# Output projection's first tile pulled forward between attention heads, and the work around it re-ordered

## The chip, the cores and the metric

The kernel runs on one core of one Trainium2 chip. The metric is the device time of the whole program in microseconds. Four compute engines work side by side, each through its own instructions in program order: TensorE (PE, with its weight loads PEld), VectorE (DVE), ScalarE (ACT) and GpSimd (POOL). SyncE (SP) only issues weight transfers. They wait for one another by counting semaphores.

## The reference, cut to what matters

Two blocks of two layers each are computed for 256 tokens of width 1024 in float32. The change lies in the first block's first layer, the attention mixer, and in the output projection behind it (shortened, with the normalisations left out):

```
z = h @ w_in
...
o_mla = blocked_causal_attention(q, k, v_mla, MLA_QK ** -0.5)         # 8 heads, rms-normed q and k, rope
o_fox = blocked_causal_attention(qf, kf, vf, FOX_DIM ** -0.5, cum_log_f)  # 8 heads, forget gates
h = h + concatenate([o_mla, o_fox]) @ w_out
h = h + sq_relu_mlp(rms_norm(h, g_mlp), w_mlp_up, w_mlp_down)
```

Each MLA query row carries a normalising factor, (mean of squares) ** -0.5, for each head. The log_sigmoid of a vector `lam` belongs to the second block, much later.

## The kernel before

Every matrix product is done in float32 by three passes: the weights are split into a high part `whi` (ACT, a copy of `raw` in a rounded format) and a low part `wlo` (DVE, `raw` minus `whi`), the activations likewise (`xhi` and `xlo`, or `chi` and `clo` for the attention's output), and TensorE adds hi·hi, hi·lo and lo·hi in one bank of `ps`. A **unit** is 8 blocks of 128x128 weights, which is one output tile of 128 features: 24 matmuls of 258 columns here. `whi` and `wlo` have 4 slots; ACT and DVE split a unit three units ahead of its use (LA = 3): the helper `ahead`, called at unit j, splits unit j + 3, and DVE's split waits for ACT's.

**The head steps.** 18 items (`items`) go through a software pipeline: 16 heads ("h", 0 to 7 fox, 8 to 15 MLA) and two small items ("d") for the first queries. In step `st` TensorE computes the scores of item st, transposes the probabilities of item st-2 (`turn`) and multiplies item st-3 by the values (`values`). DVE takes the row maximum (`peak`, L1468) and divides by the sum (`normal`, L1491), ACT takes the exponential (`exps`, L1883) and copies the transposes back (`turned`, L1913). Items use two banks of scores in turn, so scores(j) wait for the exponential of j-2. The results of a pair of heads become one block of `chi` (`high`) and `clo` (`low`, L1497).

In the same steps the MLA keys and queries are finished. `key_spread(i)` (L963) is one matmul into bank 7, which waits for DVE's `k_normed` of pair i-1 (L1454, L1458), since that still reads the bank. `q_stats` are small matmuls for the queries' sums of squares, one part each in `turn(1)` to `turn(5)`. ACT copies them out, POOL forms the mean, ACT's `query_power` raises it to -0.5 by a Ln and an Exp, and POOL refines it (`q_scale`); the first MLA item cannot be scaled before.

**The output projection** (`attn_out`, units 24 to 31). After the last scores `out_blocks` computes blocks 0 to 5 of tiles 0, 1 and 2 between the last steps, then block 6 and block 7 of the three, as these become available, then tiles 3 to 7 whole. DVE adds each tile to `h` (`dve_residual`, L552), ACT makes `xhi` and the squares from it (`act_residual`), DVE makes `xlo` (L508). The next phase, `mlp0_up`, takes block b of its first tile when `xlo` of tile b is there.

Of the kernel before, what the change touches and what calls it, by code (L numbers as in the profile page):

```python
# [19 lines left out]
F32R = mybir.dt.float32r  # L20
ACT = mybir.ActivationFunctionType
# [127 lines left out]
def program(nc, x_in, w8, w6, params_in, consts_in, rows_in, pad_in, ws_in, bs_in, out):  # L149
# [3 lines left out]
    with ctx:  # L153
# [384 lines left out]

        def dve_residual(dve, p, segs, n, c0, t):
# [255 lines left out]
        def tile_bank(t):  # L795
# [112 lines left out]
        def _(pe):  # L908
# [236 lines left out]
            def turn(j):  # L1145
# [73 lines left out]
            def out_blocks(j, kts):  # L1219

                u = p_out.unit0 + j
                o = ps[:, j % 4, 0:T1]
# [11 lines left out]
            for st in range(4, NIT + 3):  # L1234
                if st < NIT:
                    scores(st)
                if st in KEY_SPREAD:
                    key_spread(KEY_SPREAD[st])
                if st < NIT + 2:
                    turn(st - 2)  # L1240
                if items[st - 3][0] == "h":
                    values(items[st - 3][1])
                if st >= NIT:
                    j = st - NIT
                    if j < 2:
                        pe.wait_ge(ex_done, parts_done(NIT - 1 + j))
                    else:
                        pe.wait_ge(pt_done, NHD - 1)
                    out_blocks(j, range(KT - 2))
# [138 lines left out]
        def _(dve):  # L1388
# [71 lines left out]

            def peak(j):
# [8 lines left out]
                if j == 1 + HEADS:  # L1470
                    dve.wait_ge(q_scale, 6)
                    nc.vector.tensor_reduce(q_d[0:META, 0:1], q_diag[0:META, :], AX.X, ALU.add).then_inc(q_scale, 1)
# [33 lines left out]
            def step(st):  # L1506
                if st < NIT:
                    peak(st)
                if 1 <= st <= NIT:
                    normal(st - 1)  # L1510
                if st in KEY_FINAL:
# [96 lines left out]
            for _ in dve_log_sigmoid(dve, par("lam", 0, NB), half_lam[:, :], tmp[:, 0, 0:NB], tmp[:, 1, 0:NB],  # L1608
                            tmp[:, 0, NB:2 * NB], s("lam_step"), s("lam_exp_asked"), s("lam_exp")):
# [4 lines left out]

# [897 lines left out]
```

## Time and profile before

| | us |
|---|---|
| median of 3 runs | 1332.41 (1332.26 to 1333.31) |
| the profiled execution | 1332.28, span 1330.5 |
| TensorE busy | 1302.3, 98% of the span |
| head steps 4 to 17 on TensorE | 101.4 to 147.1 |
| output projection until the next phase's first tile is done | 147.1 to 177.8 |

Times within the span are counted from its first instruction. In the timeline rows the second number is how long an instruction, or a merged run of them, took; the number in brackets is the engine's idle time just before it, with the instruction that released it. Matmuls are pipelined: the next one starts before the former is finished, so their pace is read from starts.

### The profile page before, as it was taken

Reading aid. Unit: us, or ns where it says so; the run is one execution under the profiler, and the core shown is the slowest. Engines: PE = TensorE matmul, PEld = TensorE weight load, DVE = VectorE, ACT = ScalarE, POOL = GpSimd, SP = SyncE. Lnnn points to the kernel's source line nnn. Section 1 sums busy time; section 2 is a strip of 40 time slices with the busy share of each in tenths; the row PEclk is TensorE's granted clock in tenths of the full one; section 3 lists DMA queues with packets and bytes.
Section 4 is the critical chain, followed back from the end, with each engine's and each line's share of the span. In section 5 each row is a group of like instructions: output and inputs, shape, how many; then the busy total and the mean of one; then the engine's idle time right before and its main releaser. Section 6 shows DMA issues by size and latency. Waiting matters only on the chain. (4 is left out here: it accounts for less than half of the span.)

```text
span 1330.5 us, 28216 instructions
## 1 busy us (share of the span) xinstructions
PE 1302.3 (98%) x10550; PEld 1274.0 (96%) x10550; DVE 953.9 (72%) x1426; ACT 743.5 (56%) x1192; POOL 342.7 (26%) x374
## 2 busy tenths in 40 slices
PE   9998999999999999999999999999999989999997
PEld 8987899999999999999899999999999989999996
DVE  6867787655487776655455669998559898999844
ACT  5555554444343554444556556666457886666542
POOL 4632133310011233200006214343103022434311
PEclk9999999999999999999999999999999999999998
DMA  9520155555555455555545545554564445555451
GB/s 307 187 100 1 67 188 190 189 191 180 174 185 188 159 190 189 190 187 177 205 158 186 190 155 199 188 182 147 186 214 173 169 167 198 205 183 180 158 191 55
DMA packets 35370, 230.50 MB, mean 173 GB/s; under 512 B 4062, under 2 KB 5214, under 8 KB 11910
## 3 DMA queue, kind: packets, MB, share of 16 engines
q1 hardware_dynamic: 34228, 226.99, 48.6%
q10 hardware_dynamic: 1058, 2.38, 0.5%
q8 instruction: 54, 0.88, 0.3%
q14 instruction: 30, 0.25, 0.1%
HBM read 228.17 MB, written 1.05 MB: 172 GB/s over the span
## 5 line engine op out<-in xcount | busy, mean ns | idle before, releaser
L392 DVE TENSOR_TENSOR wlo<-raw,whi 128x1024 fp32r<-128x1024 f32 (+1 forms) x446 | 525.5, 1182 | 104.7 <-ACT whi L386 102.2
L427 PE MATMUL ps<-xhi,whi 128*128 128x256 f32 (+2 forms) x1920 | 542.9, 283 | 4.9 <-DVE wlo L392 3.9
L428 PE MATMUL ps<-xlo,whi 128*128 128x256 f32 (+2 forms) x1920 | 542.0, 282 | 0.0
L429 PE MATMUL ps<-xhi,wlo 128*128 128x256 f32 (+2 forms) x1920 | 540.8, 282 | 0.0
L386 ACT ACTIVATE whi<-raw 128x1024 fp32r<-128x1024 f32 (+2 forms) x444 | 446.8, 1011 | 153.3 <-PE ps L429 135.7
L427 PEld LDWEIGHTS ps<-xhi,whi 128*128 128x128 f32 x1920 | 362.4, 189 | 8.6 <-issue 5.6
L429 PEld LDWEIGHTS ps<-xhi,wlo 128*128 128x128 f32 x1920 | 362.9, 189 | 0.0
L428 PEld LDWEIGHTS ps<-xlo,whi 128*128 128x128 f32 x1920 | 360.7, 188 | 0.3
L427 PE MATMUL ps<-hhi,whi 128*128 128x256 f32 (+1 forms) x1184 | 334.3, 282 | 2.0 <-issue 0.8
L429 PE MATMUL ps<-hhi,wlo 128*128 128x256 f32 (+1 forms) x1184 | 333.2, 281 | 0.0
L428 PE MATMUL ps<-hlo,whi 128*128 128x256 f32 (+1 forms) x1184 | 333.0, 281 | 0.0
L427 PEld LDWEIGHTS ps<-hhi,whi 128*128 128x128 f32 x1184 | 223.6, 189 | 3.6 <-issue 1.9
L428 PEld LDWEIGHTS ps<-hlo,whi 128*128 128x128 f32 x1184 | 223.5, 189 | 0.0
L429 PEld LDWEIGHTS ps<-hhi,wlo 128*128 128x128 f32 x1184 | 223.4, 189 | 0.0
L534 POOL TENSOR_TENSOR ssum<-ssum,sq 128x256 f32<-128x256 f32 (+1 forms) x63 | 48.8, 774 | 393.4 <-ACT sq L515 393.4
L714 POOL TENSOR_TENSOR work<-work 128x256 f32<-128x256 f32 x48 | 66.2, 1378 | 176.5 <-ACT work L670 171.0
L552 DVE TENSOR_TENSOR h<-ps,h 128x256 f32<-128x256 f32 (+3 forms) x56 | 23.7, 424 | 115.6 <-PE ps L429 115.2
L685 ACT ACTIVATE work<-tmp,params 128x256 f32<-128x256 f32 x96 | 57.7, 601 | 87.0 <-DVE tmp L655 87.0
L628 POOL TENSOR_TENSOR hlo<-act,hhi 128x258 f32 (+1 forms) x64 | 66.7, 1042 | 119.4 <-ACT hhi L620 119.4
L503 ACT ACTIVATE xhi<-h,params 128x256 fp32r<-128x256 f32 (+1 forms) x56 | 28.6, 511 | 88.8 <-DVE h L552 83.3
L620 ACT ACTIVATE hhi<-act 128x258 fp32r<-128x258 f32 (+3 forms) x64 | 26.9, 420 | 88.1 <-DVE act L607 88.1
L646 DVE SCALAR_TENSOR_TENSOR work<-tmp,params,work 128x254 f32<-128x254 f32 x96 | 53.6, 558 | 10.4 <-DVE work L643 0.3
(339 smaller groups left out, 1338.1 us busy)
## 6 DMA issues: line engine op xcount, KB each, us to landing
raw<-w SPq DMA_DIRECT2D x182, 1024.0 KB, 4.9
raw<-w SPq DMA_DIRECT2D x40, 768.0 KB, 4.2
raw<-w SPq DMA_DIRECT2D x4, 512.0 KB, 5.4
h<-x_fm ACTq DMA_DIRECT2D x4, 272.0 KB, 5.6
out_fm<-h SPq DMA_DIRECT2D x6, 128.0 KB, 1.9
ws<-ws_src ACTq DMA_DIRECT2D x1, 512.0 KB, 3.5
bs<-bs_rows ACTq DMA_DIRECT2D x1, 512.0 KB, 5.0
consts<-constants SPq DMA_DIRECT2D x1, 508.0 KB, 10.4
```

The costliest lines, as they stand in the source:

```text
L386: nc.scalar.activation(whi[:, w, 0:n], raw[:, slot, col:col + n], ACT.Copy).then_inc(whi_done, 3 if lead else 1)
L392: nc.vector.tensor_tensor(wlo[:, w, 0:n], raw[:, slot, col:col + n], whi[:, w, 0:n].bitcast(F32), ALU.subtract).then_inc(wlo_done, 3 if fr ...
L427: nc.tensor.matmul(o, hi, xh, start=start, stop=False)
L428: nc.tensor.matmul(o, hi, xl, start=False, stop=False)
L429: mm = nc.tensor.matmul(o, lo, xh, start=False, stop=stop)
L503: nc.scalar.activation(xhi[:, kt, c0:c0 + t], h[:, kt, c0:c0 + t], ACT.Identity, scale=par(NORM_GAIN[n], kt)).then_inc(xhi_done, 1)
L534: nc.gpsimd.tensor_tensor(ssum[:, c0:c0 + t], ssum[:, c0:c0 + t], sq[:, slot, 0:t], ALU.add).then_inc(ssum_done, 1)
L620: nc.scalar.activation(hi[:, k, 0:t], src[:, j % 2, 0:t], ACT.Copy).then_inc(uhi_done, 1)
L628: nc.gpsimd.tensor_tensor(lo[:, k, 0:t], src[:, j % 2, 0:t], hi[:, k, 0:t].bitcast(F32), ALU.subtract).then_inc(ulo_done, 1)
L646: nc.vector.scalar_tensor_tensor(out=c[:, 2:SEQ], in0=x[:, 0:SEQ - 2], scalar=w0, in1=c[:, 2:SEQ], op0=ALU.mult, op1=ALU.add).then_inc(who ...
L685: nc.scalar.activation(cb[:, j % 4, :], tmp[:, j % 2, 0:SEQ], ACT.Identity, scale=par(f"f_conv_w{layer}", it * (3 * UB) + 3 * j + 2), bias ...
L714: nc.gpsimd.tensor_tensor(half[:, i % 2, :], gg[:, i % 2, :], cb[:, (2 * i + 1) % 4, :], ALU.mult).then_inc(u_done, 1)
```

## The change

1. The item list takes the first MLA head ("h", 8) before the second small item ("d", 1); the other MLA heads follow behind it.
2. `query_power` moves from ACT (Ln, Exp) to DVE (an integer first guess and two Newton steps, 8 instructions of 24 columns), in step 7. The parts of `q_stats` are done in four turns in place of five, and POOL waits for DVE's eighth instruction.
3. `key_spread` comes behind `turn` and `values` in its step, and the last one, with its `k_normed`, moves from step 7 to step 8.
4. Blocks 0 to 3 of output tile 0 run in steps 15, 16 and 17 (one, two, one), in bank 7, which the key spreads have left. Only blocks 4 and 5 stay where all six were.
5. In `dve_residual` of `attn_out` the split of the unit three ahead comes before the addition of the tile, not between the addition and `xlo`.
6. All of the `lam` log_sigmoid but its first two instructions moves behind `mlp0_up`.

```diff
+            return 7 if j == 0 else j % 4
...
                 for j in range(UB):
                     if j % segs != segs - 1:
+                        ahead(dve, split_lo, p, it, j, last)
+                    if p.name == "attn_out":
                         ahead(dve, split_lo, p, it, j, last)
                     if j % segs == segs - 1:
...
-                        nc.vector.tensor_tensor(hh, ps[:, jt % ring + (4 - ring), 0:t], hh,
+                        bank = out_bank(jt) if p.name == "attn_out" else jt % ring + (4 - ring)
+                        nc.vector.tensor_tensor(hh, ps[:, bank, 0:t], hh,
                                                 ALU.add).then_inc(tile_free, 1)
-                        ahead(dve, split_lo, p, it, j, last)
+                        if p.name != "attn_out":
+                            ahead(dve, split_lo, p, it, j, last)
                         if n != 8:
                             dve_xlo(dve, n, kt, c0, t)
...
-        items = ([("d", 0)] + [("h", i) for i in range(HEADS)] + [("d", 1)]
-                 + [("h", HEADS + i) for i in range(HEADS)])
+        items = ([("d", 0)] + [("h", i) for i in range(HEADS + 1)] + [("d", 1)]
+                 + [("h", HEADS + i) for i in range(1, HEADS)])
...
+        OUT_EARLY = {15: (0,), 16: (1, 2), 17: (3,)}
-        KEY_SPREAD = {5: 1, 6: 2, 7: 3}
-        KEY_FINAL = {4: 0, 5: 1, 6: 2, 7: 3}
+        KEY_SPREAD = {5: 1, 6: 2, 8: 3}
+        KEY_FINAL = {4: 0, 5: 1, 6: 2, 8: 3}
...
-                if 1 <= j < 6:
-                    q_stats(j - 1)
-                if j == 6:
+                for part in {1: (0,), 2: (1,), 3: (2, 3), 4: (4,)}.get(j, ()):
+                    q_stats(part)
+                if j == 5:
                     pe.wait_ge(s("q_stats_out"), 2)
...
-                if st in KEY_SPREAD:
-                    key_spread(KEY_SPREAD[st])
                 if st < NIT + 2:
                     turn(st - 2)
                 if items[st - 3][0] == "h":
                     values(items[st - 3][1])
+                if st in KEY_SPREAD:
+                    key_spread(KEY_SPREAD[st])
+                if st in OUT_EARLY:
+                    if 0 in OUT_EARLY[st]:
+                        pe.wait_ge(k_out, 4 * HEADS // 2)
+                    out_blocks(0, OUT_EARLY[st])
...
-                    out_blocks(j, range(KT - 2))
+                    out_blocks(j, range(4 if j == 0 else 0, KT - 2))
...
+            def query_power():
+
+                c, y, z, mean = s("q_power"), q_inv[:, :, :], q_neg[:, :, :], q_part[:, 0:3, :]
+                yi = y.bitcast(I32)
+                dve.wait_ge(s("q_mean"), 1)
+                nc.vector.tensor_scalar(yi, mean.bitcast(I32), 1, None, ALU.logical_shift_right).then_inc(c, 1)
+                dve.wait_ge(c, 1)
+                nc.vector.tensor_scalar(yi, yi, -1, 0x5F3759DF, ALU.mult, ALU.add).then_inc(c, 1)
+                for k in range(2):
+                    dve.wait_ge(c, 3 * k + 2)
+                    nc.vector.tensor_tensor(z, y, y, ALU.mult).then_inc(c, 1)
...
-                nc.scalar.activation(q_neg[:, :, :], q_part[:, 0:3, :], ACT.Ln).then_inc(s("q_log"), 1)
-                act.wait_ge(s("q_log"), 1)
-                nc.scalar.activation(q_inv[:, :, :], q_neg[:, :, :], ACT.Exp, scale=-0.5).then_inc(s("q_power"), 1)
...
-            pool.wait_ge(s("q_power"), 1)
+            pool.wait_ge(s("q_power"), 8)
```

How the order of instructions moves on DVE at the output projection, in the kernel before: `wlo` is the low part of a weight unit, `h` the residual sum of a tile, `xlo` the low part of that tile's activations, and `half_lam` and `params` end the log_sigmoid.

```order
L1611 TENSOR_SCALAR half_lam<-tmp 128x12 [waits lam_step]
L1612 TENSOR_SCALAR params<-params 128x24
L552 TENSOR_TENSOR h<-ps,h 128x258 [waits unit_done]
L392 TENSOR_TENSOR wlo<-raw,whi 128x1024 [waits whi_done]
L508 SCALAR_TENSOR_TENSOR xlo<-h,params,xhi 128x258 [waits xhi_done]
L552 TENSOR_TENSOR h<-ps,h 128x258 [waits unit_done]
L392 TENSOR_TENSOR wlo<-raw,whi 128x1024 [waits whi_done]
L508 SCALAR_TENSOR_TENSOR xlo<-h,params,xhi 128x258 [waits xhi_done]
```

The same place on DVE in the changed kernel:

```order
L748 SCALAR_TENSOR_TENSOR tmp<-params 128x12 [waits params_loaded]
L751 COPY half_lam<-tmp 128x12 [waits lam_step]
L393 TENSOR_TENSOR wlo<-raw,whi 128x1024 [waits whi_done]
L560 TENSOR_TENSOR h<-ps,h 128x258 [waits unit_done]
L509 SCALAR_TENSOR_TENSOR xlo<-h,params,xhi 128x258 [waits xhi_done]
L393 TENSOR_TENSOR wlo<-raw,whi 128x1024 [waits whi_done]
L560 TENSOR_TENSOR h<-ps,h 128x258 [waits unit_done]
L509 SCALAR_TENSOR_TENSOR xlo<-h,params,xhi 128x258 [waits xhi_done]
```

The sum of a tile now stands behind a split, where it stood ahead of it, and the log_sigmoid is gone from in front of the first sum. ACT's own order there is the same in both kernels, here as the changed one has it:

```order
L387 ACTIVATE whi<-raw 128x1024 [waits unit_done,raw_full1]
L504 ACTIVATE xhi<-h,params 128x258 [waits tile_free]
L516 ACTIVATE sq<-h 128x258 [waits ssum_done]
L387 ACTIVATE whi<-raw 128x1024 [waits unit_done,raw_full2]
L504 ACTIVATE xhi<-h,params 128x258 [waits tile_free]
L516 ACTIVATE sq<-h 128x258 [waits ssum_done]
```

Nothing moved here: the high part of the next unit still stands behind `xhi` and `sq` of the tile, and `xhi` waits for `tile_free`, which the sum `h` counts up.

On TensorE, steps 15 and 16 of the changed kernel (L1238 to L1240 are `out_blocks`, L1150 and L1152 scores, L1186 transposes, L1201 to L1205 values):

```order
L1238 MATMUL ps<-chi,whi 128x258 [waits olo_done,wlo_done,k_normed]
L1239 MATMUL ps<-clo,whi 128x258
L1240 MATMUL ps<-chi,wlo 128x258
L1150 MATMUL ps<-k_mla,q_mla 128x144 [waits k_normed,q_normed,exp_done]
...
L1205 MATMUL ps<-extra,v_early 128x258 [waits d_turned]
L1238 MATMUL ps<-chi,whi 128x258 [waits olo_done,wlo_done]
L1239 MATMUL ps<-clo,whi 128x258
L1240 MATMUL ps<-chi,wlo 128x258
L1238 MATMUL ps<-chi,whi 128x258 [waits olo_done]
```

In the kernel before, the scores follow the values there at once:

```order
L1191 MATMUL ps<-extra,v_main 128x258 [waits prob_t_done]
L1192 MATMUL ps<-extra,v_main 128x128
L1195 MATMUL ps<-extra,v_early 128x258 [waits d_turned]
L1140 MATMUL ps<-k_mla,q_mla 128x144 [waits k_normed,q_normed,exp_done]
L1142 MATMUL ps<-mask_r 128x128
```

So three or six matmuls of the output projection now stand ahead of the scores of items 16 and 17, and three ahead of the transposes of item 16.

## Rows read from the trace of the kernel before

**Rows 1.** Page, busy time, share of the span and instructions of each engine

```profile
PE 1302.3 (98%) x10550; PEld 1274.0 (96%) x10550; DVE 953.9 (72%) x1426; ACT 743.5 (56%) x1192; POOL 342.7 (26%) x374
```

**Rows 2.** Timeline of TensorE, head steps (start us, us, what, idle before)

```profile
106.75 0.39 PE L963 MATMUL ps<-inv,sel 128*128 128x272 f32 x1 [1.40 <-DVE k_mla L1458]
...
123.39 0.70 PE L1191 MATMUL ps<-extra,v_main 128*128 128x258 f32 x2 [2.09 <-ACT extra L1913]
...
126.89 0.41 PE L1140 MATMUL ps<-k_mla,q_mla 96*128 96x144 f32 x2
...
153.03 0.60 PE L1191 MATMUL ps<-extra,v_main 128*128 128x258 f32 x2
```

**Rows 3.** Timeline of VectorE, its waits in the head steps

```profile
112.00 0.66 DVE L1468 TENSOR_REDUCE soft<-ps 128x1 f32<-128x144 f32 x2 [1.88 <-PE ps L1142]
...
121.46 0.43 DVE L1497 TENSOR_TENSOR clo<-ps,chi 128x258 fp32r<-128x258 f32 x1 [0.76 <-ACT chi L1919]
...
123.13 0.15 DVE L1472 TENSOR_REDUCE q_d<-q_diag 16x1 f32<-16x8 f32 x1 [1.07 <-POOL q_neg L2284]
...
125.67 0.65 DVE L1468 TENSOR_REDUCE soft<-ps 128x1 f32<-128x144 f32 x2 [1.36 <-PE ps L1142]
...
127.97 0.66 DVE L1468 TENSOR_REDUCE soft<-ps 128x1 f32<-128x144 f32 x2 [0.79 <-PE ps L1142]
```

**Rows 4.** Timeline of ScalarE, its query_power

```profile
118.10 1.28 ACT L1834 ACT_TABLE_LOAD   x1
...
120.93 0.22 ACT L1836 ACTIVATE q_inv<-q_neg 128x24 f32<-128x24 f32 x1
```

**Rows 5.** Timeline of TensorE, output projection and next phase's first tile

```profile
157.63 0.28 PE L1230 MATMUL ps<-chi,wlo 128*128 128x258 f32 x1
...
160.49 0.39 PE L1228 MATMUL ps<-chi,whi 128*128 128x258 f32 x1 [1.86 <-DVE wlo L392]
...
177.53 0.39 PE L427 MATMUL ps<-xhi,whi 128*128 128x258 f32 x1
```

**Rows 6.** Timeline of VectorE, log_sigmoid, output projection, next phase

```profile
155.78 0.17 DVE L726 TENSOR_SCALAR tmp<-half_lam 128x12 f32<-128x12 f32 x1 [0.28 <-ACT half_lam L2007]
...
156.87 1.19 DVE L732 SCALAR_TENSOR_TENSOR tmp<-tmp 128x12 f32<-128x12 f32 x6
...
158.88 0.42 DVE L552 TENSOR_TENSOR h<-ps,h 128x258 f32<-128x258 f32 x1
159.22 1.22 DVE L392 TENSOR_TENSOR wlo<-raw,whi 128x1024 fp32r<-128x1024 f32 x1
160.35 0.87 DVE L508 SCALAR_TENSOR_TENSOR xlo<-h,params,xhi 128x258 fp32r<-128x258 f32 x1
161.14 0.41 DVE L552 TENSOR_TENSOR h<-ps,h 128x258 f32<-128x258 f32 x1
...
175.13 0.43 DVE L552 TENSOR_TENSOR h<-ps,h 128x258 f32<-128x258 f32 x1 [0.38 <-PE ps L1230]
...
186.15 1.23 DVE L392 TENSOR_TENSOR wlo<-raw,whi 128x1024 fp32r<-128x1024 f32 x1 [0.64 <-ACT whi L386]
```

**Rows 7.** Timeline of ScalarE, output projection and next phase

```profile
159.33 0.51 ACT L503 ACTIVATE xhi<-h,params 128x258 fp32r<-128x258 f32 x1 [2.64 <-DVE h L552]
...
160.06 1.04 ACT L386 ACTIVATE whi<-raw 128x1024 fp32r<-128x1024 f32 x1
...
185.07 1.05 ACT L386 ACTIVATE whi<-raw 128x1024 fp32r<-128x1024 f32 x1
```

**Rows 8.** Windows A:B: length, busy (x) of PE PEld DVE ACT POOL, clock, DMA

```profile
108.00:111.00 3.00, 3.00 (x12) 2.62 (x11) 2.03 (x5) 1.33 (x6) 0.00 (x0) 0.50 0.00 0
...
126.89:147.10 20.21, 17.76 (x114) 14.91 (x113) 15.86 (x54) 16.28 (x51) 2.81 (x9) 1.00 0.13 44
...
1323.00:1324.00 1.00, 0.00 (x0) 0.00 (x0) 1.00 (x2) 0.00 (x0) 0.61 (x2) 0.55 0.00 0
```

**Rows 9.** Timeline of TensorE, its last matmuls

```profile
1321.05 0.70 PE L1384 MATMUL ps<-sq,consts 128*128 128x256 f32 x2 [0.54 <-ACT sq L515]
```

More of the change, by code:

```diff
@@ L20 @@
 F32R = mybir.dt.float32r
+I32 = mybir.dt.int32
 ACT = mybir.ActivationFunctionType
@@ L535, in pool_ssum, with out_bank @@
                                     ALU.add).then_inc(ssum_done, 1)
+        def out_bank(j):
+            return 7 if j == 0 else j % 4
         def dve_residual(dve, p, segs, n, c0, t):
@@ L1221, in out_blocks @@
                 u = p_out.unit0 + j
-                o = ps[:, j % 4, 0:T1]
+                o = ps[:, out_bank(j), 0:T1]
                 pe.wait_ge(wlo_done, u + 1)
@@ L1242, in _ @@
                     values(items[st - 3][1])
+                if st in KEY_SPREAD:
[4 more added lines that the diff above has]
+                    out_blocks(0, OUT_EARLY[st])
                 if st >= NIT:
                     j = st - NIT
-                    if j < 2:
-                        pe.wait_ge(ex_done, parts_done(NIT - 1 + j))
-                    else:
+                    if j == 1:
+                        pe.wait_ge(ex_done, parts_done(NIT))
+                    if j == 2:
                         pe.wait_ge(pt_done, NHD - 1)
-                    out_blocks(j, range(KT - 2))
+                    out_blocks(j, range(4 if j == 0 else 0, KT - 2))
             for j in range(3):
@@ L1459, in k_normed @@
                                         ALU.mult).then_inc(k_out, 1)
+            def query_power():
[8 more added lines that the diff above has]
+                    nc.vector.tensor_tensor(z, y, y, ALU.mult).then_inc(c, 1)
+                    dve.wait_ge(c, 3 * k + 3)
+                    nc.vector.scalar_tensor_tensor(out=z, in0=z, scalar=-0.5, in1=mean, op0=ALU.mult,
+                                                   op1=ALU.mult).then_inc(c, 1)
+                    dve.wait_ge(c, 3 * k + 4)
+                    nc.vector.scalar_tensor_tensor(out=y, in0=z, scalar=1.5, in1=y, op0=ALU.add,
+                                                   op1=ALU.mult).then_inc(c, 1)
             def peak(j):
@@ L1471, in peak @@
                     dve.wait_ge(q_scale, 6)
+                if j == D1:
                     nc.vector.tensor_reduce(q_d[0:META, 0:1], q_diag[0:META, :], AX.X, ALU.add).then_inc(q_scale, 1)
@@ L1510, in step @@
                     normal(st - 1)
+                if st == 7:
+                    query_power()
                 if st in KEY_FINAL:
@@ L1607, in _ @@
             dve.wait_ge(s("params_loaded"), 16)
-            for _ in dve_log_sigmoid(dve, par("lam", 0, NB), half_lam[:, :], tmp[:, 0, 0:NB], tmp[:, 1, 0:NB],
-                            tmp[:, 0, NB:2 * NB], s("lam_step"), s("lam_exp_asked"), s("lam_exp")):
+            lam = dve_log_sigmoid(dve, par("lam", 0, NB), half_lam[:, :], tmp[:, 0, 0:NB], tmp[:, 1, 0:NB],
+                            tmp[:, 0, NB:2 * NB], s("lam_step"), s("lam_exp_asked"), s("lam_exp"))
+            next(lam)
+            dve_residual(dve, ph["attn_out"], 1, 1, C1, T1)
+            dve_rstd(dve, 1, C1, T1, ph["mlp0_up"])
+            dve_mlp_up(dve, ph["mlp0_up"], C1, T1)
+            for _ in lam:
                 pass
@@ L1613, in _ @@
                                     ALU.mult).then_inc(s("gate_bias_done"), 1)
-            dve_residual(dve, ph["attn_out"], 1, 1, C1, T1)
-            dve_rstd(dve, 1, C1, T1, ph["mlp0_up"])
-            dve_mlp_up(dve, ph["mlp0_up"], C1, T1)
             dve_residual(dve, ph["mlp0_down"], 4, 2, C1, T1)
@@ L1829, in to @@
                     done[0] += 1
-            def query_power():
-                act.wait_ge(s("q_mean"), 1)
-                nc.scalar.activation(q_neg[:, :, :], q_part[:, 0:3, :], ACT.Ln).then_inc(s("q_log"), 1)
-                act.wait_ge(s("q_log"), 1)
-                nc.scalar.activation(q_inv[:, :, :], q_neg[:, :, :], ACT.Exp, scale=-0.5).then_inc(s("q_power"), 1)
             def roots(n):
@@ L1904, in turned @@
                                          ACT.Copy).then_inc(pt0_done, 1)
-                if j == 5:
+                if j == 4:
                     nc.scalar.activation(q_part[:, :, :], ps[:, 6, 2 * P:2 * P + 4 * HEADS].rearrange(
@@ L1926, in step @@
                     turned(st - 2)
-                if st == 7:
-                    query_power()
                 if st >= 3 and second(st - 3) and items[st - 3][1] < HEADS:
```

## The prediction

> **What bounds the kernel now.** I read the page's busy times first: TensorE is busy 1302.3 of 1330.5 us [rows 1]. A change of order can only win what TensorE stands idle or runs slowly, and it loses as soon as it makes new idle time. So I went to the timeline of TensorE over the edited stretch and looked for its waits. In the head steps there are several: 1.40 us for the key norms at 106.75 and 2.09 us for ACT's copy at 123.39 [rows 2]. Then I looked at what DVE waits for in the same steps [rows 3], since it does more small work there than the others, and at what holds ACT: two table loads, from 118.10 to 121.15 [rows 4]. From 147.1 on TensorE runs without a gap until 158.6, waits 1.86 us for the low weight part of the fourth tile, and has no gap again until the next phase's first tile is done [rows 5]. The reader should keep the last view in mind: between 160.49 and 177.53 TensorE issues 5 tiles of 24 matmuls and 7 blocks of 3, 141 in 17.04 us, which is 0.121 us each and **2.9 us for a tile**. Whatever feeds it there must be faster than that.
>
> **The change, part by part.**
>
> *Split before the sum in the output projection (part 5).* Before, DVE adds tile j, splits unit j+3 while ACT makes xhi and the squares of tile j and the high part of unit j+4, and then makes xlo. Its pace was 161.14 - 158.88 = 2.26 us a tile [rows 6], less than TensorE's 2.9. The rows of order show that ACT's order is untouched: the high part of unit j+4 stands behind xhi of tile j, which waits for the sum of tile j. With the split of unit j+4 now ahead of the sum of tile j+1, everything stands in one chain: sum(j), xhi(j), squares(j), high(j+4), low(j+4), sum(j+1). From starts in the rows: sum to xhi 159.33 - 158.88 = 0.45; xhi to high part 160.06 - 159.33 = 0.73 [rows 6, 7]; high part to the low part that waits for it 186.15 - 185.07 = 1.08 [rows 6, 7]; low part to DVE's next instruction 160.35 - 159.22 = 1.13 [rows 6]. The sum is **3.39 us a tile, slower than TensorE's 2.9**. No row of before shows the chain closed like this, but each link of it stands in one, and nothing in it is optional.
>
> What it costs is read at the last block of the next phase's first tile, which needs xlo of tile 7. Before: tile 0 is finished at 157.63 + 0.28 = 157.91 and that block starts at 177.53 [rows 5], 19.6 us later, the stall of 1.86 us included. After: the first sum follows tile 0 at once (0.05), seven periods are 23.7, then sum to xhi 0.45, xhi 0.51, xlo 0.87, and 0.07 for two hand-overs: 25.7 us. **Loss 6.1 us.** Most of it is no stall between tiles: TensorE itself would be through tile 7 about 17 us after tile 0, and then waits for xlo of tiles 5, 6 and 7, each a period behind the other. For tiles 4 to 7 the low weight parts come 0.5 us late each, and the rest, twice about 3 us, is waited ahead of the last two blocks.
>
> *The log_sigmoid moved (part 6).* Its 3.1 us from 155.78 to 158.88 stood in front of the first sum and of the split that TensorE waits 1.86 us for [rows 5, 6]. Gone from there, the split of the fourth tile is done before tile 0 is. That win of 1.86 is already inside the 6.1, since I counted from one end to the other. Behind mlp0_up the same 3 us are hidden by splits three units ahead, 8.7 us of TensorE; without that cover they would cost 3.1.
>
> *Head steps up to the second MLA head (parts 1 to 3).* I count in DVE's idle time, because its work there is fixed and nearly without a gap. Before, from 106.7 to the peak of head 9 at 127.97, it waits 1.88 + 0.76 + 1.07 + 1.36 + 0.79 = 5.86 us [rows 3]: for scores behind the late key spread, for ACT behind its table loads, for POOL's scale behind the same, and for two scores that follow from it. The table loads go entirely, 3.0 us of ACT. Into DVE's line come the 8 new instructions. Nothing in the trace is a shift or an integer product, but the chain of small dependent ones nearest to it takes 1.19 / 6 = 0.2 us each [rows 6], so 1.6; the bounds are nothing more than 1.0 and 2.4 us. New waits: the key spread of pair 1 now stands behind a transpose and a values product, which puts it about 0.65 us behind the point where DVE wants it, and I leave 1.1 us of the waits for scores, because scores follow exponentials and those are not faster. 5.86 - 1.6 - 0.65 - 1.1 = **2.5 us won**, bounds 1.0 and 4.2 (none of the new waits). In this the clock counts too: after the wait of 1.40 us TensorE ran at half clock from 108 to 111 [rows 8]. With the spread at the end of the step that wait is gone, and I take it that the fall is gone with it.
>
> *Heads 9 to 15 and the early blocks (part 4).* From 126.89 to 147.10 TensorE is idle 20.21 - 17.76 = 2.45 us [rows 8]. Four blocks of 0.36 us, 1.44 us in all, are put there, and go from behind 147.1. They do not simply fill gaps: the scores of items 16 and 17 stand behind them and DVE's peak waits for scores, so part of the 1.44 pushes the chain. Step by step, the first block is taken up by the gap before the next values, the next two push by 0.7 to 0.8, the last falls into a gap: about 0.6 won. The short item now between heads 8 and 9 lets ACT catch up, where it ran two full exponentials ahead of a copy, for another 0.8. **1.4 us won**, bounds 0 and 2.45.
>
> Both together bring the last values product, 153.03 before [rows 2], forward by **3.9 us**, and behind it the order is fixed up to tile 0's end.
>
> *The clock.* In the stretch of loss TensorE would be idle for 3 us, do 0.36 us, be idle for 3 us again. At the end of the program the granted clock had fallen from 2.4 to 1.2 GHz by 1323 to 1324, 2 us after the last matmuls [rows 8, 9], and in the head steps it fell behind an idle stretch of 1.40. The row at half clock covers 3.00 us of a busy TensorE, so it gave up 1.5 us, and with its edges somewhat more. I add **1.8 us** for one such fall; bounds 0 and 3.
>
> Sum, against the profiled execution's own 1332.28, which is 0.13 below the median: 1332.3 + 6.1 - 3.9 + 1.8 = 1336.3; I say 1336.2.
>
> Two rules of the skill bear on this. The Trainium skill, "ScalarE: Activation LUTs", section "What ACT_TABLE_LOAD costs", gives 1283 ns for a load and about as much again for a drain, 2.66 us for a switch. The load agrees with 1.28 here, but the next instruction starts at once, so no row here shows the drain; by the page's figure the two loads would be worth 5.3 us of ACT and not 2.6, and the head steps could win up to 2.7 us more. The Trainium skill, "TensorE: Matmul & The Clock Gate", section "Architectural detail", says that ScalarE and VectorE are strict first in, first out, which speaks against this change: ACT cannot start the next high part ahead of a waiting xhi. The trace agrees, ACT idles 2.64 us ahead of xhi with the next high part behind it.
>
> **The rivals.**
>
> *The chain does not bind; the change is faster.* If ACT had the next high part ready, the period would stay under 2.9, and only the wins would be left: 1332.3 - 3.9 - 1.86 = 1326.5. The deciding point is a period of 2.9 us: three links of 0.45, 1.08 and 1.13 are hand-overs that can't shrink by 0.5 together, so I give it 1 in 20. The same side is reached if the head steps win more than 6.1 us; their upper bounds are 4.2 + 2.45 = 6.65. 1 in 20.
>
> *The clock does not fall.* The wait of 2.09 us that ended at 123.39 was not followed by half-rate matmuls [rows 2], so an idle stretch alone does not bring the fall each time. Then 1334.4, within 0.2%. 1 in 4.
>
> *The head steps win less.* If the clock still falls among them (1.5), or DVE's integer instructions cost 2.4, or the early blocks only push, 3.9 becomes about 2: 1338.2. 3 in 20.
>
> *The forecast* itself has 1 in 2.
>
> **How the numbers follow.** What a measurement of this kernel can tell from no change is about 0.2%, 2.7 us. Slower than 1335.1: forecast and the last rival, 0.65. Within: the rival without a fall, 0.25. Faster than 1329.7: 0.10. The range leaves out the two cases on the fast side and the far end of the last rival: low 6.1 - 5.2 + 0 = 0.9, high 6.1 - 2.2 + 1.8 = 5.7, so 1333.2 to 1338.0.
>
> **What would show it.** In the trace after: sums of the output projection 3.4 us apart, not 2.26; TensorE waits of about 0.5 us for the low weight part ahead of tiles 5, 6 and 7, and two of about 3 us for xlo in the next phase's first tile; half clock right behind. No Ln and no table load in the head steps; eight small DVE instructions of 0.2 us; the last values product near 149.1. The prediction is wrong if the sums come 2.9 us apart or less, or if the last values product stands earlier than 147 or later than 151.

## The result, and the profile after

| | us |
|---|---|
| before, median of 7 runs | 1332.41 (1330.17 to 1333.31) |
| after, median of 7 runs | 1337.43 (1336.28 to 1338.86) |
| ratio after / before | 1.0042, 95% interval 1.003 to 1.0053 |
| the profiled execution of after | 1338.36, span 1336.6 |

The change makes the kernel 5.0 us slower. The forecast was 1336.2, with a range of 1333.2 to 1338.0: the sign is right and the time lies in the range, but the step from before was put at 3.8 us, which is less than the interval of the ratio allows (4.0 to 7.1).

VectorE in the timeline of the changed kernel, from the first split to the third tile (start, duration, what, idle before). It answers to [rows 6]:

```profile
155.54 1.23 DVE L393 TENSOR_TENSOR wlo<-raw,whi 128x1024 fp32r<-128x1024 f32 x1 [1.23 <-ACT whi L387]
156.76 0.43 DVE L560 TENSOR_TENSOR h<-ps,h 128x258 f32<-128x258 f32 x1
157.76 0.49 DVE L509 SCALAR_TENSOR_TENSOR xlo<-h,params,xhi 128x258 fp32r<-128x258 f32 x1 [0.58 <-ACT xhi L504]
159.02 1.23 DVE L393 TENSOR_TENSOR wlo<-raw,whi 128x1024 fp32r<-128x1024 f32 x1 [0.77 <-ACT whi L387]
160.16 0.42 DVE L560 TENSOR_TENSOR h<-ps,h 128x258 f32<-128x258 f32 x1
161.16 0.49 DVE L509 SCALAR_TENSOR_TENSOR xlo<-h,params,xhi 128x258 fp32r<-128x258 f32 x1 [0.58 <-ACT xhi L504]
162.42 1.23 DVE L393 TENSOR_TENSOR wlo<-raw,whi 128x1024 fp32r<-128x1024 f32 x1 [0.77 <-ACT whi L387]
163.56 0.42 DVE L560 TENSOR_TENSOR h<-ps,h 128x258 f32<-128x258 f32 x1
...
180.56 0.42 DVE L560 TENSOR_TENSOR h<-ps,h 128x258 f32<-128x258 f32 x1
```

The sums are 3.40 us apart, to the last one at 180.56. DVE now waits twice in each tile, 0.58 us for `xhi` and 0.77 us for `whi`, where it had hardly a gap before: it isn't the engine that sets the pace. ScalarE in the same place, which answers to [rows 7], closes the circle:

```profile
160.62 0.51 ACT L504 ACTIVATE xhi<-h,params 128x258 fp32r<-128x258 f32 x1 [1.63 <-DVE h L560]
161.04 0.40 ACT L516 ACTIVATE sq<-h 128x258 f32<-128x258 f32 x1
161.35 1.04 ACT L387 ACTIVATE whi<-raw 128x1024 fp32r<-128x1024 f32 x1
```

ScalarE waits 1.63 us for `h`, DVE's split waits for `whi`, and `h` stands behind the split. The links, by starts: 160.16 to 160.62, to 161.35, to 162.42, to 163.56, which is 0.46 + 0.73 + 1.07 + 1.14 = 3.40.

TensorE from the last values product to the statistics of the next phase (L472), which answers to [rows 5] and to the last row of [rows 2]:

```profile
151.84 0.60 PE L1201 MATMUL ps<-extra,v_main 128*128 128x258 f32 x2
...
163.75 0.36 PE L1238 MATMUL ps<-chi,whi 128*128 128x258 f32 x1 [0.27 <-issue]
167.15 0.36 PE L1238 MATMUL ps<-chi,whi 128*128 128x258 f32 x1 [0.27 <-issue]
...
178.70 0.39 PE L428 MATMUL ps<-xhi,whi 128*128 128x258 f32 x1 [2.37 <-DVE xlo L509]
182.10 0.58 PE L428 MATMUL ps<-xhi,whi 128*128 128x258 f32 x1 [2.77 <-DVE xlo L509]
182.91 0.42 PE L428 MATMUL ps<-xhi,whi 128*128 128x258 f32 x1
...
187.34 0.60 PE L472 MATMUL ps<-ssum,consts 128*128 128x258 f32 x2
```

The big waits are not where the tiles are computed but ahead of the last two blocks of the next phase's first tile, 2.37 and 2.77 us. The matmul behind 182.91 takes 0.42 us and not 0.28: the clock is down. Windows of the same profile (length, busy of PE, PEld, DVE, ACT, POOL, then the granted clock, DMA share, GB/s) show it twice, in the head steps and behind the loss; they answer to [rows 8]:

```profile
104.00:105.00 1.00, 1.00 (x9) 0.82 (x10) 0.96 (x3) 0.00 (x0) 0.86 (x2) 0.74 0.00 0
...
106.00:107.00 1.00, 1.00 (x5) 0.81 (x4) 0.97 (x4) 0.95 (x5) 0.84 (x1) 0.50 0.00 0
...
180.00:186.00 6.00, 3.90 (x18) 3.91 (x19) 2.69 (x4) 3.05 (x4) 0.64 (x1) 0.50 0.41 137
```

And VectorE in the head steps: the key norms' wait for the spread, and the first two of the eight instructions that replace Ln and Exp.

```profile
111.68 0.49 DVE L1468 SCALAR_TENSOR_TENSOR k_mla<-early,params,ps 64x272 f32<-64x272 f32 x1 [1.59 <-PE ps L973]
...
118.85 0.17 DVE L1480 TENSOR_SCALAR q_inv<-q_part 128x24 int32<-128x24 int32 x1
119.06 0.18 DVE L1482 TENSOR_SCALAR q_inv<-q_inv 128x24 int32<-128x24 int32 x1
```

Five marks let every profile be split into stretches: the first `q_stats` matmul, the last values product, the first sum, the last block of the next phase's first tile, and the statistics matmul behind it. Start times in us, of all profiled executions (the labels are those of the experiments below). The last column has the microseconds in which the granted clock was at or near half:

| profile | q_stats | last values | first sum | last block | statistics | clock fell to half |
|---|---|---|---|---|---|---|
| before | 100.00 | 153.03 | 158.88 | 177.53 | 180.88 | 108 to 111 |
| e5 (before) | 102.22 | 154.40 | 160.25 | 180.45 | 183.78 | 125 to 129, 163 to 167 |
| e10 (before) | 101.75 | 157.40 | 163.26 | 181.92 | 185.26 | 109 to 119 |
| after | 101.50 | 151.84 | 156.76 | 182.10 | 187.34 | 105 to 108, 180 to 186 |
| e9 (after) | 101.32 | 149.99 | 154.90 | 180.24 | 185.85 | 179 to 185 |
| e1 | 101.96 | 150.64 | 155.55 | 174.21 | 177.55 | none |
| e2 | 101.34 | 154.39 | 161.38 | 186.72 | 192.10 | 110 to 112, 185 to 191 |
| e3 | 100.84 | 150.26 | 155.18 | 180.53 | 186.40 | 180 to 186 |
| e4 | 102.56 | 151.22 | 156.13 | 173.99 | 177.32 | none |
| e6 | 100.93 | 150.33 | 155.24 | 173.12 | 176.44 | none |
| e7 | 100.63 | 151.61 | 156.52 | 174.38 | 177.70 | 124 to 127 |
| e8 | 100.56 | 152.90 | 157.81 | 175.68 | 179.01 | 108 to 114 |
| e11 | 101.10 | 153.31 | 158.23 | 176.89 | 180.23 | 124 to 128 |
| e12 | 102.49 | 151.15 | 156.06 | 179.25 | 184.10 | 180 to 182 |

The last column tells of 101 to 192 us alone. What lies behind the statistics is 1149.1 to 1149.8 us in every one of them, so nothing of the change acts there; the log_sigmoid in its new place costs nothing that can be seen.

### The profile page after: what moved, and what is told of

Read it like the earlier page. It is cut to its first block and busy times, and to the rows that moved or that the text cites. A ratio compares the mean times of both kernels' runs of the same rounds, so it can differ in the third digit from the quotient of the medians.

```text
span 1336.6 us, 28222 instructions
## 1 busy us (share of the span) xinstructions
PE 1305.1 (98%) x10550; PEld 1275.7 (95%) x10550; DVE 952.5 (71%) x1434; ACT 740.0 (55%) x1188; POOL 344.3 (26%) x374
## 5 line engine op out<-in xcount | busy, mean ns | idle before, releaser
(340 smaller groups left out, 1334.2 us busy)
```

## The experiments

They were run in three groups, each beside its own runs of the kernel before: e1 to e4 (before 1332.13, 13 runs), e5 to e8 (1333.31, 19 runs), e9 to e12 (1333.15, 23 runs).

**e1, the sum first again.** The changed kernel without its part 5.

```diff
-                    if p.name == "attn_out":
-                        ahead(dve, split_lo, p, it, j, last)
...
-                        if p.name != "attn_out":
-                            ahead(dve, split_lo, p, it, j, last)
+                        ahead(dve, split_lo, p, it, j, last)
```

> The changed kernel with one part undone: in the output projection DVE again adds the tile before it splits the unit three ahead. All else is as changed. If the closed chain of 3.4 us a tile is the loss (my theory), the sums come 2.3 us apart until they meet TensorE's pace, the two waits of about 3 us for xlo in the next phase's first tile go, the half clock behind them goes too, and one wait of about 1.1 us for the low part of the fourth tile comes back: about 8 us faster than the changed kernel, 1329 to 1330 us, ratio to before 0.997 to 0.998. If the loss came from the moved log_sigmoid or from the early blocks, this would stay near 1337.

Measured: 1328.16 (1326.39 to 1328.91), ratio 0.996, interval 0.9946 to 0.9974. The sums are 2.26 us apart again:

```profile
155.55 0.43 DVE L558 TENSOR_TENSOR h<-ps,h 128x258 f32<-128x258 f32 x1 [2.45 <-PE ps L1237]
155.90 1.22 DVE L393 TENSOR_TENSOR wlo<-raw,whi 128x1024 fp32r<-128x1024 f32 x1
157.03 0.87 DVE L509 SCALAR_TENSOR_TENSOR xlo<-h,params,xhi 128x258 fp32r<-128x258 f32 x1
157.82 0.41 DVE L558 TENSOR_TENSOR h<-ps,h 128x258 f32<-128x258 f32 x1
```

First sum to last block takes 18.66 us instead of 25.34, and the clock stays up behind it. One place in DVE's order is worth 9.3 us, and all the rest of the change together is a win of 4.0 us.

**e2, the split first alone.** The kernel before with part 5 and nothing else.

```diff
+                    if p.name == "attn_out":
+                        ahead(dve, split_lo, p, it, j, last)
...
-                        ahead(dve, split_lo, p, it, j, last)
+                        if p.name != "attn_out":
+                            ahead(dve, split_lo, p, it, j, last)
```

> The kernel before with this one part done: the split three ahead stands before the sum of the tile in the output projection. The log_sigmoid is still in front of the first sum. Theory: the chain runs from the end of that first split, about 160.0, seven periods of 3.4 and 1.9 more: the next phase's first tile ends near 185.7 and not 177.5, 8 us later, and the clock falls behind it for another 1.5: 1341 to 1342 us. Rival, that the order of DVE costs nothing by itself: 1332.

Measured: 1341.55 (1339.91 to 1343.0), ratio 1.0062, interval 1.0047 to 1.0076; that is 9.4 us more than before. First sum to last block is 25.34 us, to a hundredth what the whole change has, and the clock falls behind it too. The loss belongs to part 5 alone.

**e3, no early blocks.** The changed kernel with all six blocks of tile 0 where they were.

```diff
-        OUT_EARLY = {15: (0,), 16: (1, 2), 17: (3,)}
+        OUT_EARLY = {}
...
-                    out_blocks(j, range(4 if j == 0 else 0, KT - 2))
+                    if j == 0:
+                        pe.wait_ge(k_out, 4 * HEADS // 2)
+                    out_blocks(j, range(KT - 2))
```

> The changed kernel with blocks 0 to 3 of output tile 0 back behind the last scores, still in bank 7. Theory: the four blocks were worth 0.6 us in the head steps, so this is 0.6 slower than the changed kernel, about 1338.0. Rival A, they fill gaps entirely: 1.4 slower. Rival B, they only push the scores: no difference, or faster. The last values product tells it in the trace more closely than the time does.

Measured: 1337.23 (1336.19 to 1338.6), ratio 1.0032, interval 1.0021 to 1.0043. By the time alone the kernel without the early blocks is 0.2 us faster and not 0.6 slower, which is below what the time can tell. By the stretches, `q_stats` to last values product is 49.42 us. In the first profile of after it is 50.34, but with the clock down for a while; so e6 and e9 were made for this.

**e4, the split first for one tile.** Part 5 kept for tile 0, where DVE waits for it anyway, and the old order for the other seven.

```diff
-                    if p.name == "attn_out":
+                    if p.name == "attn_out" and j == 0:
...
-                        if p.name != "attn_out":
+                        if p.name != "attn_out" or j > 0:
```

> The changed kernel with the split ahead of the sum for the first tile alone; from the second tile on DVE adds first and splits then. Theory: the wait of 1.1 us for the fourth tile's low part that the plain order has goes as well, and nothing else changes against it: 1328 to 1329 us, 9 us faster than the changed kernel and about 1 us faster than with the plain order. Rival, the first closed link delays the second tile's split as well: equal to the plain order.

Measured: 1327.01 (1325.83 to 1328.26), ratio 0.9953, interval 0.994 to 0.9967. It has the lowest median of all versions and is faster than both kernels. The split of unit 3 is done before the first sum, so the wait for it on TensorE is gone (0.93 us in e1), and the circle doesn't close: first sum to last block is 17.86 us.

**e5, the kernel before, a second profile.** No edit.

> The kernel before, unchanged, for a second profile. Its first profile had the first q_stats matmul at 100.0 us, all others (changed kernels) at 100.8 to 102.6. Theory A, that the start depends on when the first weight transfers land and the first profile was a lucky one: this one has it at 100.8 to 102.6 too, and the last values product 53.0 behind it, if the clock falls in the head steps as in the first. Theory B, that the changed program starts later for a reason of its own: this one has it at 100.0 again, within 0.3.

Measured: 1335.31, one run. Its first `q_stats` matmul came 2.22 us later. `q_stats` to last values product took 52.18 us instead of 53.03. The clock stayed up at the place where it had fallen in the first profile, but it fell at two others: from 125 to 129, behind the wait of 2.10 us for ACT's copy, and from 163 to 167, behind TensorE's wait for `wlo`, which made first sum to last block 20.20 us instead of 18.65. The first row is VectorE's instruction that waits 1.88 us in [rows 3], the other two are windows:

```profile
112.55 0.65 DVE L1468 TENSOR_REDUCE soft<-ps 128x1 f32<-128x144 f32 x2 [0.22 <-PE ps L1142]
```

```profile
126.00:128.00 2.00, 2.00 (x10) 1.63 (x9) 1.07 (x6) 0.25 (x1) 0.00 (x0) 0.50 0.00 0
163.00:166.00 3.00, 3.00 (x16) 3.00 (x16) 3.00 (x4) 2.52 (x6) 0.70 (x1) 0.50 0.88 317
```

On the start theory A holds: the 100.0 of the first profile is not the program's. And the two profiles together give the old head steps without any fall, though neither has them whole: from `q_stats` to the values product behind the wait for ACT's copy 21.71 us here (123.93 - 102.22; 21.73 in e11), and from there to the last values product 29.64 us in the first profile (153.03 - 123.39; 29.66 in e2 and e10). An estimate from these is 51.35 us.

**e6, e4 without the early blocks.** The edit of e3, on e4.

> The best version so far (e4, 1327.0) without the early blocks of tile 0. Theory A, that the four early blocks fill gaps for about half of their 1.44 us: the last values product comes 49.4 behind the first q_stats matmul instead of 48.7, and the time is 1327.7 to 1327.8. Theory B, that they only push the scores and are worth nothing, as the times of e3 against the changed kernel look: 48.7 and 1327.0.

Measured: 1328.14 (1326.1 to 1328.63), ratio 0.9957, interval 0.9942 to 0.9971, beside 0.9953 for e4. `q_stats` to last values product is 49.40 us against 48.66 in e4, both with the clock up: the early blocks win 0.74 us of the 1.44 that they hold. The times agree with that and don't prove it.

**e7, the power on ScalarE.** e4 with Ln and Exp back in step 7.

```diff
-            def query_power():
...
+                act.wait_ge(s("q_mean"), 1)
+                nc.scalar.activation(q_neg[:, :, :], q_part[:, 0:3, :], ACT.Ln).then_inc(s("q_log"), 1)
+                act.wait_ge(s("q_log"), 1)
+                nc.scalar.activation(q_inv[:, :, :], q_neg[:, :, :], ACT.Exp, scale=-0.5).then_inc(s("q_power"), 1)
...
-            pool.wait_ge(s("q_power"), 8)
+            pool.wait_ge(s("q_power"), 1)
```

> e4 (1327.0) with query_power back on ScalarE as Ln and Exp. Theory A, that ScalarE's 3.0 us of Ln, Exp and table loads are on the path of the first MLA head and DVE's eight instructions cost less than they free: the first q_stats matmul to the last values product grows from 48.7 to 50 or 51, and the time to 1328.5 to 1329.5, more if the clock falls behind a longer idle stretch. Theory B, that DVE is the engine that bounds the head steps, so that 1.6 us off it are worth as much as 3 us on ScalarE: 48.7 and 1327.0.

Measured: 1330.3 (1328.87 to 1331.86), ratio 0.9973, interval 0.9963 to 0.9983. `q_stats` to last values product grows from 48.66 to 50.98 us. TensorE's timeline shows where, and a window of the same profile shows that the clock fell behind it:

```profile
122.40 0.70 PE L1201 MATMUL ps<-extra,v_main 128*128 128x258 f32 x2 [2.99 <-ACT extra L1930]
```

```profile
124.00:127.00 3.00, 3.00 (x24) 2.54 (x21) 1.58 (x8) 1.48 (x7) 0.00 (x0) 0.50 0.00 0
```

The same values product waits 0.84 us in e4. It starts 21.77 us behind `q_stats` here and 20.25 in e4, so 1.5 us are lost before the clock falls. The other 0.8 us are lost between it and the scores of head 9, at half clock. So 1.7 us more on DVE (eight times 0.21) for 3.0 us less on ScalarE is a win of 1.5 us by the order, and of 2.3 with the fall. The medians differ by 3.3 us; the mean clock of these eleven executions is 0.995 to 0.997, and 0.998 in all of e4. Theory A, with its clause on the clock.

**e8, the key spreads ahead again.** e4 with the call of `key_spread` back in front of `turn` and `values`.

```diff
+                if st in KEY_SPREAD:
+                    key_spread(KEY_SPREAD[st])
                 if st < NIT + 2:
                     turn(st - 2)
                 if items[st - 3][0] == "h":
                     values(items[st - 3][1])
-                if st in KEY_SPREAD:
-                    key_spread(KEY_SPREAD[st])
```

> e4 (1327.0) with the key spreads ahead of turn and values again, in the same steps. Theory A, that TensorE's wait for the key norms (1.40 us before) is back and with it a stretch at half clock in the head steps: the first q_stats matmul to the last values product is 50 to 51 instead of 48.7, time 1328.5 to 1329.5. Theory B, that the fall of the clock does not hang on this wait: the wait comes back, the clock stays, 49.0 to 49.5 and 1327.3 to 1327.8.

Measured: 1328.17 (1326.89 to 1332.09), ratio 0.996, interval 0.9947 to 0.9974. The wait is back, and in the profiled execution (1330.35) the clock fell right behind it for over 6 us:

```profile
107.32 0.39 PE L973 MATMUL ps<-inv,sel 128*128 128x272 f32 x1 [1.40 <-DVE k_mla L1472]
```

```profile
108.00:114.00 6.00, 6.00 (x25) 5.51 (x25) 2.54 (x8) 1.82 (x6) 0.07 (x1) 0.50 0.00 0
```

But its nine executions differ: two with a mean granted clock of 0.994 and 0.995 took 1332.09 and 1330.35 us, and the three with 0.998 took 1327.01 to 1328.23, which is close to e4's time; the other four lie between 1326.89 and 1330.10. Neither theory as written: wait and fall together cost 3.7 us in the profile (52.34 us from `q_stats` to last values product against 48.66). By the times of the three, the wait in itself costs little, but no profile of this version without the fall shows it. That the fall comes in a part of the executions only is read from their mean clocks. In the 18 executions of e1, e4 and e6, which have the spread at the end, the mean clock was 0.997 or 0.998 each time. The place of the spread isn't all of it: e7 has it at the end too, and had 0.995 to 0.997.

**e9, the changed kernel, a second profile.** No edit.

> The changed kernel, unchanged, for a second profile. In its first one the granted clock fell to 1.2 GHz at 104.3 us, and from the first q_stats matmul to the last values product it took 50.3 us; e1, e3, e4 and e6, with the same head steps there or nearly, had no such fall and took 48.7 or 49.4. Theory A, that the fall in the head steps comes in some executions only, and not in most of the changed kernel's (five of its seven had a mean clock of 0.995, two of 0.994): no fall before 150 us now, 48.7, one fall behind the loss, and a time of 1336.5 to 1338. Theory B, that the changed kernel brings the fall at 104 each time: 50.3 again, mean clock 0.994.

Measured: 1336.87, mean clock 0.995. No fall in the head steps, and 48.67 us from `q_stats` to last values product. The wait of the key norms is 0.26 us, where the first profile had 1.59:

```profile
109.83 0.49 DVE L1468 SCALAR_TENSOR_TENSOR k_mla<-early,params,ps 64x272 f32<-64x272 f32 x1 [0.26 <-PE ps L973]
```

Theory A: five of the seven executions of after had 0.995, as this one, and two 0.994, the profiled one among them.

**e10, the kernel before, a third profile.** No edit.

> The kernel before, a third profile. The first had its first q_stats matmul at 100.0 and a fall of the clock at 108, the second had it at 102.2 and a fall at 163. Theory A, that both the start (when the first transfers land) and the place of the fall differ between executions of one program: q_stats between 100.5 and 102.5, and 52.2 to the last values product without a fall there, 53.0 with one. Theory B, that 100.0 is usual for this program: 99.8 to 100.3.

Measured: 1336.4. `q_stats` at 101.75, as theory A has it, but 55.65 us to the last values product, outside what was expected: the clock fell at 109, behind the wait for the key norms, and stayed down for 10 us (0.54 in the microsecond from 109, 0.84 in the one from 119):

```profile
110.00:118.00 8.00, 8.00 (x32) 7.09 (x33) 4.85 (x15) 2.45 (x10) 0.00 (x0) 0.50 0.00 1
```

**e11, the log_sigmoid moved alone.** The kernel before with part 6 only.

```diff
-            for _ in dve_log_sigmoid(dve, par("lam", 0, NB), half_lam[:, :], tmp[:, 0, 0:NB], tmp[:, 1, 0:NB],
+            lam = dve_log_sigmoid(dve, par("lam", 0, NB), half_lam[:, :], tmp[:, 0, 0:NB], tmp[:, 1, 0:NB],
...
+            next(lam)
+
+            dve_residual(dve, ph["attn_out"], 1, 1, C1, T1)
+            dve_rstd(dve, 1, C1, T1, ph["mlp0_up"])
+            dve_mlp_up(dve, ph["mlp0_up"], C1, T1)
+            for _ in lam:
                 pass
...
-            dve_residual(dve, ph["attn_out"], 1, 1, C1, T1)
-            dve_rstd(dve, 1, C1, T1, ph["mlp0_up"])
-            dve_mlp_up(dve, ph["mlp0_up"], C1, T1)
```

> The kernel before with part 6 of the change alone, the log_sigmoid behind mlp0_up. Theory A, that it delays the first sum by 0.9 us behind tile 0's end and with it the split that TensorE waits 1.86 us for: the wait falls to 0.9 to 1.0, the first sum of tile 0 to the last block of the next phase's first tile takes as long as before plus nothing, time 0.9 less than before. Theory B, that the wait is set by ScalarE's high part and stays at 1.86: no difference.

Measured: 1330.49 (1329.12 to 1332.63), ratio 0.9983, interval 0.9972 to 0.9993. TensorE's wait for the low part:

```profile
159.84 0.39 PE L1228 MATMUL ps<-chi,whi 128*128 128x258 f32 x1 [0.93 <-DVE wlo L392]
```

It was 1.86 [rows 5] and is 0.93. The last values product to the last block takes 23.58 us, 0.92 less than before's 24.50: theory A. In its head steps the clock fell as well, from 124 to 128, behind the wait for ACT's copy. The rest of the 2.7 us between the medians is not explained by it; a shorter wait may also be followed by a fall of the clock less often, but the one profile can't show that.

**e12, the high part ahead of the squares.** The changed kernel with one more swap, on ScalarE in the output projection.

```diff
-                    ahead(act, split_hi, p, it, j, last)
+                    if p.name != "attn_out" or j == 0:
+                        ahead(act, split_hi, p, it, j, last)
...
                             act_gained(act, n, kt, c0, t)
+                        if p.name == "attn_out" and j < UB - 1:
+                            ahead(act, split_hi, p, it, j + 1, last)
                         act_square(act, n, kt, jt % 2, c0, t)
```

> The changed kernel with ScalarE's high part of the next unit ahead of the squares of the tile in the output projection. Theory A, that sum, xhi, squares, high part, low part and the next sum form one closed chain: taking the squares (0.31 us from start to start) out of it brings the sums from 3.40 to 3.09 us apart, the first sum to the last block of the next phase's first tile from 25.3 to 23.2, and the time from 1337.4 to about 1335.2. Theory B, that DVE or TensorE sets the pace and not the closed chain: the sums stay 3.4 apart, 1337.4.

Measured: 1334.44 (1332.77 to 1335.94), ratio 1.0006, interval 0.9996 to 1.0016. With the squares out of the circle the sums are 3.09 to 3.10 us apart (3.09 expected), and first sum to last block is 23.19 us (23.2 expected):

```profile
158.02 1.23 DVE L393 TENSOR_TENSOR wlo<-raw,whi 128x1024 fp32r<-128x1024 f32 x1 [0.46 <-ACT whi L387]
159.16 0.42 DVE L560 TENSOR_TENSOR h<-ps,h 128x258 f32<-128x258 f32 x1
160.16 0.49 DVE L509 SCALAR_TENSOR_TENSOR xlo<-h,params,xhi 128x258 fp32r<-128x258 f32 x1 [0.58 <-ACT xhi L504]
161.11 1.22 DVE L393 TENSOR_TENSOR wlo<-raw,whi 128x1024 fp32r<-128x1024 f32 x1 [0.46 <-ACT whi L387]
162.26 0.42 DVE L560 TENSOR_TENSOR h<-ps,h 128x258 f32<-128x258 f32 x1
```

DVE's wait for `whi` went from 0.77 to 0.46, the very 0.31 taken out. The time fell by 3.0 us, 0.8 more than the 2.2 of the period, since the clock was down for 3 us behind it and not for 6 to 7. This is the strongest evidence for the closed chain: a pace set by DVE or by TensorE alone would not follow an edit on ScalarE, and ScalarE alone doesn't set it either, since it waits 1.63 us for `h` in each tile of the changed kernel.

## How the prediction fared, and which step failed

**The chain of part 5: right.** Predicted 3.39 us a tile from four links, measured 3.40, with each link within 0.01. From the first sum to the last block 25.34 us, against 25.6 by the prediction; the 0.3 is mostly the `xlo`, which was taken at 0.87 [rows 6] and takes 0.49 here. So the loss is 5.8 and not 6.1 (last values product to last block 30.26 against 24.50). The waits stand where they were forecast, a little smaller: 0.27 us ahead of tiles 5 to 7 and not 0.5, 2.37 and 2.77 ahead of the last blocks and not 3. Part 6 inside it: e11 shows that the log_sigmoid alone stood for 0.93 of the wait of 1.86, the split first at tile 0 for the rest (e4).

**The clock behind the loss: right.** Last block to statistics: 5.24 us in the first profile and 5.61 in the second, 3.35 before, so 1.9 to 2.3 against 1.8. It fell in all four profiles of the kernels with the 3.40 period (after, e9, e2, e3). The rival in which it doesn't fall is refuted there.

**The head steps: this is the step that failed.** The prediction has "5.86 - 1.6 - 0.65 - 1.1 = 2.5 us won", and 1.4 behind it, 3.9 in all. The first term of the 5.86, DVE's 1.88 us "for scores behind the late key spread", was made for 1.66 us of it by the clock and not by the order: TensorE ran at half clock from 108 to 111 just ahead of it, and in e5, with the clock up there, the same instruction waits 0.22. Without a fall in either kernel the old head steps take 51.35 us (the estimate at e5) and the new ones 48.67 (e9), so the order wins 2.7 us and not 3.9. With one fall in both, 53.03 against 50.34, it is 2.7 again. Of these, 1.0 us lie ahead of the scores of head 9 (25.21, which is 21.71 and the 3.50 from 123.39 to 126.89 in [rows 2], against 24.24; predicted 2.5) and 1.7 behind (26.14 against 24.43; predicted 1.4). The small terms were close: DVE's eight instructions cost 8 x 0.21 = 1.7 (predicted 1.6), the new waits up to head 9 are 0.26 for the spread and 0.94 for its scores (predicted 0.65 and 1.1), and the early blocks win 0.74 (e6 against e4; predicted 0.6).

What the 1.88 stood for is a fall of the clock, and the text said of it: "With the spread at the end of the step that wait is gone, and I take it that the fall is gone with it." In the profiled execution it was not gone: the clock fell 3 us earlier in the program, at 104 to 105, though in the 11 us ahead of it TensorE had no wait longer than 0.41 us. This is the last rival's first branch ("if the clock still falls among them"), and its 1.5 us are 50.34 - 48.67 = 1.67. In e9, without that fall, the win over the first profile of before is 53.03 - 48.67 = 4.4: 2.7 by the order and 1.7 by the clock.

**The base of the sum: a total that was near the median by luck.** The step is: "Sum, against the profiled execution's own 1332.28, which is 0.13 below the median". In that execution the first `q_stats` matmul stood at 100.00, and in the other 13 profiles, four of them of kernels with the old code up to there, it stands at 100.56 to 102.56, in the middle at 101.34: 1.3 us early. And the clock fell in its head steps, which cost 53.03 - 51.35 = 1.7 us. The two nearly cancel in the total, but the prediction counted most of the 1.7 as a win once more and left the early start in. From `q_stats` to the statistics it has 80.88 + 4.0 = 84.9 us: e9 took 84.53 and the first profile of after 85.84. Put at the middle start, 101.3 + 84.9 + 1149.3 behind + 1.8 around the span, it makes 1337.3, and the median of after is 1337.43. That agreement is in part luck, since the loss was put 0.3 too high and the win over this one execution 0.5 too low.

Like for like, the measured terms are 5.8 for the loss, 2.7 for the order of the head steps and 1.9 to 2.3 for the clock behind the loss: 5.0 to 5.4 us slower, and the medians differ by 5.0. If a usual execution of before pays for a fall in its head steps, it should be less than that; how much it pays can't be told from the medians. All three profiles of it have one there, which cost 1.7, 0.8 (52.18, e5) and 4.3 us (55.65, e10).

What stays open: why the start moves by up to 2.5 us. In before ScalarE waited 2.40 us for a weight transfer at 30 us, in after 3.75 and in e5 5.19, and what follows is late by about that difference; whether the memory or the queue is the reason was not tried. Nor can it be said from these runs what makes the clock fall in one execution of a program and not in the next.

## What to carry to other kernels

Before an instruction is moved ahead of another on one engine, write down who waits for whom around the whole loop. If the moved one waits for an engine that itself waits for the one it was moved past, the loop becomes one serial chain and its period is the sum of all links (here 3.40 us, with both engines waiting in each tile); e4 shows that the same move is a win at the first tile, where the chain isn't closed. An order that wins (here 5.1 us, e4) can hide inside a change that loses, so try the parts one by one. And take the start and the clock of the one profiled execution apart before it serves as the base of a sum: a total near the median can be two deviations that cancel. Nor is a wait next to a stretch at half clock to be booked on the order before a second profile has shown it with the clock up (1.88 us and 0.22).

## What the runs showed of the hardware that was not expected

The granted clock falls from 2.4 to 1.2 GHz at different places in executions of the same program, and for different lengths: in three profiles of the kernel before for 3 to 4 us at 108, for as long at 125 and once more at 163, and for 10 us at 109. The same wait is followed by a fall in one execution and not in the next: the one of 1.4 us for the key norms was in the first profile and in e2, e8 and e10, and not in e5 and e11; the one of 2.1 us for ACT's copy was in e5 and e11, and not in the first profile. In the first profile of after a fall came without any wait over 0.41 us. The spread of the kernel before goes with the clock. Of its 55 executions beside the experiments, the 15 with a mean granted clock of 0.997 or 0.998 have a median of 1331.5 us, the 16 with 0.996 one of 1332.3, the 8 with 0.995 one of 1334.2, and the 16 with 0.994 or less one of 1335.5. The kernels with the key spread at the end and the sum first (e1, e4, e6) never left 0.997 to 0.998 in 18 executions; e7, which differs from e4 in the power on ScalarE and its wait of 2.99 us, had 0.995 to 0.997 in 11. So part of their win against the median of before is a clock that stays up.

An `xlo` of 128x258 on VectorE is listed with 0.87 us where it follows the split without a gap and with 0.49 where it follows a wait; the next instruction starts 0.79 or 0.40 us behind it. On 128x24 elements an integer shift, an integer product with sum and a float product all take 0.17 to 0.18 us, one each 0.21 us.
